# A two-block transformer on one core: the shared values' projection moved from behind the shared keys into the second attention

## The chip, the cores and the metric

One core of a Trainium2 chip runs the whole program in one launch. The metric is device time in microseconds (us); the kernel before takes 2057.99 us, the median of three runs (2056.74 to 2058.36). TensorE multiplies matrices, ScalarE and VectorE work elementwise, SyncE issues the weight transfers.

## The reference

A first block (two layers of gated branches) gives `x`, 256 tokens of width 1024 in float32. The second block, cut to what matters:

```python
def second_block(x, ...):
    h = x
    for layer in range(2):
        h = h + 0.5 * swiglu(rmsnorm(h, ffn1_norm[layer]), ...)
        hn = rmsnorm(h, mix_norm[layer])
        if layer == 0:
            h = h + mixer_a(hn, a_w_qkv, a_w_o, pos)
        else:
            h = h + mixer_b(hn, b_w_q, b_w_o, *shared, pos)
        h = h + 0.5 * swiglu(rmsnorm(h, ffn2_norm[layer]), ...)
        if layer == 0:
            shared = shared_kv(h, kv_norm, kv_w, pos)
    return rmsnorm(h, final_norm)

def shared_kv(h_stream, kv_norm, kv_w, pos):
    kv = rmsnorm(h_stream, kv_norm) @ kv_w       # 1024 x 2048, keys then values
    k, v = partial_rotary(kv[0], pos), kv[1]     # 16 heads of 64
```

`mixer_b` is causal attention over these keys and values with queries of its own (with 256 tokens there is one block of keys, so no selection), and `swiglu` is `(silu(h @ w_gate) * (h @ w_up)) @ w_down` with a hidden width of 2816. The shared keys and values come from `h` after layer 0; layer 1's first FFN starts from the same `h` under another norm.

## The kernel before, in words

**Weights.** All weights come as slots of 128 x 1024 numbers, in the order of use, through a ring of five buffers. A slot is loaded into `raw` (SyncE, once the slot five before it is used up), ScalarE copies it rounded into `w_hi` (line 1296), and VectorE subtracts to get the rest, `w_lo` (line 1808). Each product is made of three: high by high, high by low, low by high (lines 530 to 532). In the code of ScalarE and VectorE `split(c + AHEAD)` prepares slot c + 3, and `splits` several.

**Order.** There is no scheduler: the order on every engine is that of the code, and semaphores hold an engine at an instruction until another has counted up to a number. Whatever stands behind a waiting instruction on its engine waits too.

**Projection to tokens.** A block is four slots for 512 output columns. `wide_slot` multiplies one slot for both token tiles (twelve products of 512 columns), `wide` half of it, for one tile, into one accumulator bank per tile.

**Boundaries.** The residual stream is in `xt`, as four units (token tile x half of the width). At a boundary each unit is finished, turned by TensorE (`turn_unit`, line 914), multiplied by the norm's gains by VectorE (`gain_unit`, line 2212), rounded by ScalarE into the high part (`high_unit`, line 1512) and completed by VectorE with the low part (`low_unit`, line 2221). The row factor of the norm is applied later, to the results. Set 2 is for the shared keys and values (`kv_hi`, `kv_lo`, which lie in channels 4 to 11 of `g_hi`, `g_lo`), set 3, from the same `xt`, for layer 1's first FFN (`h_hi`, `h_lo`).

**Shared keys and values** (`keys_values`). Behind the boundary's first block of keys (k0) come a second block of keys (k1) and two of values (v0, v1). A key block is scaled by ScalarE (`take_tok`, line 1588), rotated by VectorE (`rope`, lines 2302 to 2305), turned by TensorE (`turn_qk`, line 1011) and copied out by ScalarE (`take_qk`, line 1595). A block of values is copied out, scaled, by VectorE (`take_values2`, line 2312). The four turned units of set 3 lie among these slots. Then follows the first block of FFN 2, which waits for all four:

```python
            keys_values()
            pe.wait_ge(v_ready, 3)
            pe.wait_ge(unit_lo, 4 * UNITS)
            wide_block(start["ffn2"], (0, 1))
```

**Second attention** (`attention_b`). Behind the queries' two blocks stand eight units of two heads. For each: scores (`scores2`, lines 1021 and 1022), bias and maximum on VectorE (`softmax2`, from line 2322), exponentials on ScalarE (`exps2`, lines 1603 and 1605), normalising on VectorE (`normalize2`, lines 2332 to 2336), the probabilities' transposes (`turn2`, line 1033), their copy by ScalarE (`take_turned2`, line 1611), products with the values (`values2`, line 1044), and the result's high part by ScalarE (`heads_high`, line 1615) and low part by VectorE (`heads_low`, line 2341). A unit's transposes wait until the unit before is through its low part. From unit 2 on, a unit's products stand in the middle of a slot of the output projection (`wo_slot`), and its transposes behind one. Units 0 and 1 have no projection around them.

Of the kernel before, what the change touches and what calls it, by code (L numbers as in the profile page):

```python
# [25 lines left out]
D = 1024  # L26
KD = D // P
BR = 512
# [8 lines left out]
AHEAD = 3  # L37
SEG = 3 * P
BLOCK = 4
UNITS = 4  # L40
# [46 lines left out]
def build(nc, weights, x_in, ctx_in, cols_in, consts_in, filter_consts_in, layer_in, filter_in, lam_in, tail_in, out):  # L87
# [8 lines left out]
    start = {}  # L96
# [22 lines left out]
    for p in (0, 2):  # L119
        start[f"pass{p}_merge"] = start[f"pass{p}"] + MERGE_AT  # L120
        start[f"pass{p}_wo"] = start[f"pass{p}"] + MERGE_AT + MERGE_SLOTS
    tail = [("ffn0", FFN_SLOTS), ("qkv", 24), ("wo0", 8), ("ffn1", FFN_SLOTS), ("kv", 16),
            ("ffn2", FFN_SLOTS), ("q1", 8), ("wo1", 8), ("ffn3", FFN_SLOTS)]
# [11 lines left out]
    with ctx:  # L135
# [392 lines left out]
        def _(pe):  # L528
# [606 lines left out]
            def keys_values():  # L1135

                c = start["kv"]
                k0, k1, v0, v1 = range(c, c + 16, BLOCK)
                wide_slot(k1, 0, (2, 3), kv_hi, kv_lo)
                turn_unit(3, 0, 6)  # L1140
                wide_slot(k1 + 1, 1, (2, 3), kv_hi, kv_lo)
                turn_qk(4, (0, 1))
                wide_slot(k1 + 2, 2, (2, 3), kv_hi, kv_lo)
                turn_unit(3, 1, 7)
                wide_slot(k1 + 3, 3, (2, 3), kv_hi, kv_lo)
                turn_unit(3, 2, 4)
                pe.wait_ge(qk_ready, 10)
                wide_slot(v0, 0, (0, 1), kv_hi, kv_lo)
                turn_unit(3, 3, 5)
                wide_slot(v0 + 1, 1, (0, 1), kv_hi, kv_lo)  # L1150
                turn_qk(5, (2, 3))
                wide_block(v0, (0, 1), 2, 4, kv_hi, kv_lo)
                pe.wait_ge(qk_ready, 12)
                wide_block(v1, (2, 3), 0, 4, kv_hi, kv_lo)

            def attention_b():

                qb = start["q1"] + BLOCK
# [7 lines left out]
                scores2(1, 2)  # L1166
                turn2(1, 0)

                values2(1, 0)
                scores2(1, 3)  # L1170
                turn_qk(7, (2, 3))
                turn2(1, 1)

                values2(1, 1)
                scores2(1, 4)
                turn2(1, 2)
                pe.wait_ge(qk_ready, 16)

                def values_scores(unit):
                    values2(1, unit)  # L1180
                    if unit + 3 < 8:
                        scores2(1, unit + 3)
                for i in range(6):
                    wo_slot(1, i, lambda: values_scores(i + 2))
                    if i + 3 < 8:
                        turn2(1, i + 3)
# [80 lines left out]
            keys_values()  # L1267
            pe.wait_ge(v_ready, 3)
            pe.wait_ge(unit_lo, 4 * UNITS)
            wide_block(start["ffn2"], (0, 1))  # L1270
            pe.wait_ge(v_ready, 4)
# [10 lines left out]
        def _(act):  # L1282
# [1478 lines left out]
```

## Time and profile before

| | |
|---|---|
| median of three runs | 2057.99 us |
| the profiled execution's own time | 2057.02 us |
| its span, first to last instruction | 2055.2 us |
| TensorE busy, of the span | 1983.5 us, 97% |
| VectorE, ScalarE busy | 1285.1 us (63%), 978.6 us (48%) |
| mean granted TensorE clock | 0.988 of full |
| TensorE on the chain that ended last | 88% |

Times in the trace count from the span's start. In a timeline a row gives an instruction's start and length; a bracket gives how long its engine stood idle ahead of it and whose work ended that. Consecutive instructions of an engine overlap a little, so the distance between two starts is what one of them costs. The granted clock is 1 at full speed and 0.5 at the lower of two levels; a stretch's figure is the mean over it. The shared keys and values stand at 1549 to 1595, the second attention at 1795 to 1856, behind it the boundary to the last FFN.

### The profile page before, as it was taken

How to read it: one execution, taken by the hardware profiler on the slowest of the kernel's cores; microseconds unless marked ns; L12 is line 12 of the kernel's file. 1: busy time of each engine (PE TensorE's matmuls, PEld its weight loads, DVE VectorE, ACT ScalarE, POOL GpSimd, SP SyncE). 2: the span in 40 equal slices, each digit the busy share in tenths (PEclk: the TensorE clock that was granted, in tenths of full speed). 3: DMA queues.
4: the chain of work that ended last, by engine and by line, in shares of the span. 5: the costliest groups of instructions: out<-in, count | busy, mean ns of one | idle time of the engine just before them, and what ended most of it. 6: DMA issues, size and time to landing. Idle time of an engine off the chain costs nothing.

```text
span 2055.2 us, 29618 instructions
## 1 busy us (share of the span) xinstructions
PE 1983.5 (97%) x12606; PEld 1717.9 (84%) x12606; DVE 1285.1 (63%) x1752; ACT 978.6 (48%) x1457; POOL 13.4 (1%) x18
## 2 busy tenths in 40 slices
PE   6999999999999999999989999999999999989998
PEld 3699999899998989999978887678888888768887
DVE  3777756887644777765565556755557555676555
ACT  1364444464333645534454446654445444565444
POOL 2000000000000000000000000000000000000000
PEclk9999999999999999999999999999999999999999
DMA  8544455434577443355545554345555555525654
GB/s 313 193 154 144 144 185 164 145 130 137 175 251 252 161 161 126 131 173 184 164 136 191 186 174 164 114 156 191 186 186 171 188 191 186 180 76 166 191 186 144
DMA packets 95491, 351.99 MB, mean 171 GB/s; under 512 B 10624, under 2 KB 10752, under 8 KB 94592
## 3 DMA queue, kind: packets, MB, share of 16 engines
q1 hardware_dynamic: 94032, 341.09, 50.2%
q0 software_dynamic: 1040, 7.37, 0.9%
q8 instruction: 100, 1.64, 0.3%
q10 hardware_dynamic: 288, 1.64, 0.2%
q14 instruction: 31, 0.25, 0.0%
HBM read 349.01 MB, written 1.05 MB: 170 GB/s over the span
## 4 chain that ended last, share of the span: by engine, by line
PE 88%; DVE 6%; ACT 3%; DMA 3%; issue 1%; SPq 0%; DVEq 0%; ACTq 0%
PE PS L530 26%; PE PS L532 25%; PE PS L531 25%; DMA raw<-weights 3%; DVE w_lo L1808 2%; ACT w_hi L1296 1%; PE PS L822 1%; PE PS L803 1%; PE PS L608 1%; PE PS L717 1%; PE PS L951 1%; PE PS L736 1%; PE PS L914 1%; PE PS L1033 1%; PE PS L726 0%
## 5 line engine op out<-in xcount | busy, mean ns | idle before, releaser
L1808 DVE TENSOR_TENSOR w_lo<-raw,w_hi 128x1024 fp32r<-128x1024 f32 x600 | 727.6, 1223 | 407.0 <-ACT w_hi L1296 405.4
L1296 ACT ACTIVATE w_hi<-raw 128x1024 fp32r<-128x1024 f32 x600 | 624.9, 1056 | 418.6 <-DMA raw<-weights 414.0
L530 PE MATMUL PS<-h_hi,w_hi 128*128 128x256 f32 x1568 | 454.6, 290 | 7.9 <-DVE h_lo L1826 3.9
L531 PE MATMUL PS<-h_lo,w_hi 128*128 128x256 f32 x1568 | 445.0, 284 | 0.0
L532 PE MATMUL PS<-h_hi,w_lo 128*128 128x256 f32 x1568 | 444.8, 284 | 0.0
L530 PE MATMUL PS<-w_hi,h_hi 128*128 128x512 f32 (+1 forms) x1024 | 388.8, 380 | 8.7 <-DVE h_lo L2171 6.5
L532 PE MATMUL PS<-w_hi,h_lo 128*128 128x512 f32 (+1 forms) x1024 | 380.0, 371 | 0.0
L531 PE MATMUL PS<-w_lo,h_hi 128*128 128x512 f32 (+1 forms) x1024 | 379.3, 370 | 0.0
L530 PEld LDWEIGHTS PS<-h_hi,w_hi 128*128 128x128 f32 x1568 | 301.7, 192 | 23.3 <-issue 16.9
L531 PEld LDWEIGHTS PS<-h_lo,w_hi 128*128 128x128 f32 x1568 | 302.1, 193 | 0.9 <-issue 0.7
L532 PEld LDWEIGHTS PS<-h_hi,w_lo 128*128 128x128 f32 x1568 | 301.8, 192 | 0.0
L530 PEld LDWEIGHTS PS<-w_hi,h_hi 128*128 128x128 f32 x1024 | 193.8, 189 | 44.9 <-issue 11.7
L532 PEld LDWEIGHTS PS<-w_hi,h_lo 128*128 128x128 f32 x1024 | 193.6, 189 | 33.6
L531 PEld LDWEIGHTS PS<-w_lo,h_hi 128*128 128x128 f32 x1024 | 194.0, 189 | 31.7 <-issue 1.2
L530 PE MATMUL PS<-w_hi,g_hi 128*128 128x512 f32 (+1 forms) x512 | 200.5, 392 | 2.2 <-issue 1.3
L532 PE MATMUL PS<-w_hi,g_lo 128*128 128x512 f32 (+1 forms) x512 | 196.4, 384 | 0.0
L531 PE MATMUL PS<-w_lo,g_hi 128*128 128x512 f32 (+1 forms) x512 | 196.1, 383 | 0.0
L530 PEld LDWEIGHTS PS<-w_hi,g_hi 128*128 128x128 f32 x512 | 96.3, 188 | 22.7 <-issue 4.3
L530 PE MATMUL PS<-g_hi,w_hi 128*128 128x256 f32 x384 | 111.5, 290 | 3.2 <-DVE g_lo L2136 1.6
L532 PEld LDWEIGHTS PS<-w_hi,g_lo 128*128 128x128 f32 x512 | 96.3, 188 | 19.2
L531 PEld LDWEIGHTS PS<-w_lo,g_hi 128*128 128x128 f32 x512 | 96.4, 188 | 17.3
L532 PE MATMUL PS<-g_hi,w_lo 128*128 128x256 f32 x384 | 109.4, 285 | 0.0
(258 smaller groups left out, 1879.8 us busy)
## 6 DMA issues: line engine op xcount, KB each, us to landing
raw<-weights SPq DMA_DIRECT2D x642, 512.0 KB, 3.4
x<-weights SPq DMA_DIRECT2D x6, 512.0 KB, 10.7
layer<-layer_in POOLq DMA_DIRECT2D x2, 1280.0 KB, 11.3
consts<-consts_in POOLq DMA_DIRECT2D x1, 1184.0 KB, 10.2
arena<-filter_consts_in ACTq DMA_DIRECT2D x1, 1024.0 KB, 8.8
cx<-ctx_in POOLq DMA_DIRECT2D x1, 1024.0 KB, 8.5
x<-x_in POOLq DMA_DIRECT2D x1, 1024.0 KB, 13.4
out<-arena SPq DMA_DIRECT2D x4, 256.0 KB, 2.0
```

The costliest lines, as they stand in the source:

```text
L530: pe.matmul(dst, hi, m_hi_, start=first, stop=False, **kw)
L531: pe.matmul(dst, hi, m_lo_, start=False, stop=False, **kw)
L532: return pe.matmul(dst, lo, m_hi_, start=False, stop=last, **kw)
L608: mm = pe.matmul(PS[32 * j:32 * j + 32, bank, 0:T], c_act[:, 4 * half + j, :], w[:, j * T:(j + 1) * T], start=(half == 0), stop=(half == 1))
L717: mm = pe.matmul(PS[:, SCORES + m, g * T:(g + 1) * T], q[s, h, qt * P:(qt + 1) * P], k[s, base + h, :], start=True, stop=True)
L736: mm = pe.matmul(PS[:, HEADS_OUT + qt, h * P:(h + 1) * P], mixw_t[:, h % 2, j, qt * P:(qt + 1) * P], v[:, t, h * P:(h + 1) * P], start=(j ...
L803: mm = pe.matmul(PS[:, [0, HEADS_OUT][n] + f, :], dft[:, t, f * P:(f + 1) * P], u_tok[:, t, :], start=(t == 0), stop=(t == 1))
L822: mm = pe.matmul(PS[:, [TURN, MISC][c // 2], (c % 2) * T:(c % 2 + 1) * T], yspec[:, a_, c * P:(c + 1) * P], idft[:, a_, :], start=(a_ == 0 ...
L914: mm = pe.transpose(PS[:, bank, j * P:(j + 1) * P], xt[:, t, kk * P:(kk + 1) * P], const("ident"))
L951: mm = pe.transpose(PS[:, 2 * (b % 2), o:o + P], act_f[:, t, f * P:(f + 1) * P], const("ident"))
L1296: nc.scalar.activation(w_hi[:, r, :], raw[:, r, :], ACT.Copy).then_inc(w_hi_ready, 1)
L1808: V.tensor_tensor(w_lo[:, r, :], raw[:, r, :], f32(w_hi[:, r, :]), ALU.subtract).then_inc(w_lo_ready, 1)
```

## The change

Three things are done. The values' two blocks (8 slots) leave the place behind the keys and stand in the second attention: v0 behind the queries' second block, with the transposes of unit 0 and of the queries among its slots, and v1 slot by slot around the products and scores of units 0 to 3. All output slots thereby move back: units 4 to 7 are in slots 0 to 3, and slots 4 and 5 are plain. The four units of set 3 are turned, gained and rounded earlier, among the second block of keys alone. The first block of FFN 2 follows these keys directly, and the transposes of the second keys stand inside it. The weights' order in memory follows.

```diff
-    tail = [("ffn0", FFN_SLOTS), ("qkv", 24), ("wo0", 8), ("ffn1", FFN_SLOTS), ("kv", 16),
-            ("ffn2", FFN_SLOTS), ("q1", 8), ("wo1", 8), ("ffn3", FFN_SLOTS)]
+    tail = [("ffn0", FFN_SLOTS), ("qkv", 24), ("wo0", 8), ("ffn1", FFN_SLOTS), ("kv", 8),
+            ("ffn2", FFN_SLOTS), ("q1", 8), ("kv_v", 8), ("wo1", 8), ("ffn3", FFN_SLOTS)]
...
-            def keys_values():
-
-                c = start["kv"]
-                k0, k1, v0, v1 = range(c, c + 16, BLOCK)
+            def keys_and_first_block():
+
+                k1, f0 = start["kv"] + BLOCK, start["ffn2"]
+                turn_unit(3, 0, 6)
+                turn_unit(3, 1, 7)
                 wide_slot(k1, 0, (2, 3), kv_hi, kv_lo)
-                turn_unit(3, 0, 6)
+                turn_unit(3, 2, 4)
                 wide_slot(k1 + 1, 1, (2, 3), kv_hi, kv_lo)
                 turn_qk(4, (0, 1))
+                turn_unit(3, 3, 5)
                 wide_slot(k1 + 2, 2, (2, 3), kv_hi, kv_lo)
-                turn_unit(3, 1, 7)
                 wide_slot(k1 + 3, 3, (2, 3), kv_hi, kv_lo)
-                turn_unit(3, 2, 4)
                 pe.wait_ge(qk_ready, 10)
-                wide_slot(v0, 0, (0, 1), kv_hi, kv_lo)
-                turn_unit(3, 3, 5)
-                wide_slot(v0 + 1, 1, (0, 1), kv_hi, kv_lo)
+                pe.wait_ge(unit_lo, 4 * UNITS)
+                wide_block(f0, (0, 1), 0, 2)
                 turn_qk(5, (2, 3))
-                wide_block(v0, (0, 1), 2, 4, kv_hi, kv_lo)
+                wide_block(f0, (0, 1), 2, 4)
                 pe.wait_ge(qk_ready, 12)
-                wide_block(v1, (2, 3), 0, 4, kv_hi, kv_lo)
 
             def attention_b():
 
-                qb = start["q1"] + BLOCK
+                qb, v0 = start["q1"] + BLOCK, start["kv_v"]
+                v1 = v0 + BLOCK
                 wide_slot(qb, 0, (2, 3))
                 turn_qk(6, (0, 1))
                 wide_slot(qb + 1, 1, (2, 3))
@@ -1164,26 +1163,34 @@
                 scores2(1, 1)
                 wide_slot(qb + 3, 3, (2, 3))
                 scores2(1, 2)
+
+                pe.wait_ge(qk_ready, 14)
+                wide_slot(v0, 0, (0, 1), kv_hi, kv_lo)
                 turn2(1, 0)
-
-                values2(1, 0)
-                scores2(1, 3)
+                wide_slot(v0 + 1, 1, (0, 1), kv_hi, kv_lo)
                 turn_qk(7, (2, 3))
-                turn2(1, 1)
-
-                values2(1, 1)
-                scores2(1, 4)
-                turn2(1, 2)
+                wide_block(v0, (0, 1), 2, 4, kv_hi, kv_lo)
                 pe.wait_ge(qk_ready, 16)
 
                 def values_scores(unit):
                     values2(1, unit)
                     if unit + 3 < 8:
                         scores2(1, unit + 3)
+
+                for unit in range(4):
+                    c = v1 + unit
+                    slot_ready(c)
+                    wide(c, unit, 0, 2, kv_hi, kv_lo)
+                    if unit == 0:
+                        pe.wait_ge(v_ready, 3)
+                    values_scores(unit)
+                    wide(c, unit, 1, 3, kv_hi, kv_lo).then_inc(w_used, 1)
+                    turn2(1, unit + 1)
+                pe.wait_ge(v_ready, 4)
                 for i in range(6):
-                    wo_slot(1, i, lambda: values_scores(i + 2))
-                    if i + 3 < 8:
-                        turn2(1, i + 3)
+                    wo_slot(1, i, lambda: values_scores(i + 4) if i < 4 else None)
+                    if i < 3:
+                        turn2(1, i + 5)
...
-            keys_values()
-            pe.wait_ge(v_ready, 3)
-            pe.wait_ge(unit_lo, 4 * UNITS)
-            wide_block(start["ffn2"], (0, 1))
-            pe.wait_ge(v_ready, 4)
+            keys_and_first_block()
...
-            def keys_values():
-
-                c = start["kv"]
-                k0, k1, v0, v1 = range(c, c + 16, BLOCK)
+            def keys_and_first_block():
+
+                k0, f0 = start["kv"], start["ffn2"]
+                k1 = k0 + BLOCK
                 take_tok(4, k0, (0, 1), 3)
-                splits(k1, 2)
                 high_unit(3, 0)
+                split(k1 + AHEAD)
+                high_unit(3, 1)
+                split(k1 + 1 + AHEAD)
                 take_qk(4, k[:, 0:4, :], (0, 1))
+                high_unit(3, 2)
                 split(k1 + 2 + AHEAD)
-                high_unit(3, 1)
+                high_unit(3, 3)
                 split(k1 + 3 + AHEAD)
-                high_unit(3, 2)
                 take_tok(5, k1, (2, 3), 3)
-                split(v0 + AHEAD)
-                high_unit(3, 3)
-                split(v0 + 1 + AHEAD)
+                splits(f0, 2)
                 take_qk(5, k[:, 4:8, :], (2, 3))
-                splits(v0 + 2, 2)
-                splits(v1, 4)
-                splits(start["ffn2"], 4)
+                splits(f0 + 2, 2)
...
+                split(v0 + AHEAD)
                 take_turned2(1, 0)
-                heads_high(1, 0)
                 exps2(1, 2)
+                split(v0 + 1 + AHEAD)
                 take_qk(7, q[:, 4:8, :], (2, 3))
-                take_turned2(1, 1)
-                heads_high(1, 1)
-                exps2(1, 3)
-                wo = start["wo1"]
-                for unit in range(2, 8):
-                    take_turned2(1, unit)
-                    split(wo + unit - 2 + AHEAD)
+                splits(v0 + 2, 2)
+                for unit in range(8):
+                    if unit >= 1:
+                        take_turned2(1, unit)
+                    split((v1 + unit if unit < 4 else wo + unit - 4) + AHEAD)
                     heads_high(1, unit)
-                    if unit + 2 < 8:
+                    if 1 <= unit < 6:
                         exps2(1, unit + 2)
-                split(wo + 6 + AHEAD)
+                splits(wo + 4, 3)
...
-            def keys_values():
-
-                c = start["kv"]
-                k0, k1, v0, v1 = range(c, c + 16, BLOCK)
+            def keys_and_first_block():
+
+                k0, f0 = start["kv"], start["ffn2"]
+                k1 = k0 + BLOCK
+                gain_unit(3, 0, 6)
                 rope(4)
                 split(k1 + AHEAD)
-                gain_unit(3, 0, 6)
+                gain_unit(3, 1, 7)
+                low_unit(3, 0)
                 split(k1 + 1 + AHEAD)
-                low_unit(3, 0)
+                gain_unit(3, 2, 4)
+                low_unit(3, 1)
                 split(k1 + 2 + AHEAD)
-                gain_unit(3, 1, 7)
-                split(k1 + 3 + AHEAD)
-                low_unit(3, 1)
-                gain_unit(3, 2, 4)
-                rope(5)
-                split(v0 + AHEAD)
                 gain_unit(3, 3, 5)
                 low_unit(3, 2)
-                split(v0 + 1 + AHEAD)
+                split(k1 + 3 + AHEAD)
                 low_unit(3, 3)
-                splits(v0 + 2, 2)
-                take_values2(v0, (0, 1), 0, 3)
-                splits(v1, 4)
-                take_values2(v1, (2, 3), 1, 3)
-                splits(start["ffn2"], 4)
+                rope(5)
+                splits(f0, 4)
...
-
+                rope(7)
+                split(v0 + AHEAD)
                 softmax(2)
-                rope(7)
+                split(v0 + 1 + AHEAD)
                 normalize2(1, 1)
-                heads_low(1, 0)
-                softmax(3)
-                normalize2(1, 2)
-                heads_low(1, 1)
-                wo = start["wo1"]
-                for unit in range(2, 8):
-                    if unit + 2 < 8:
+                splits(v0 + 2, 2)
+                take_values2(v0, (0, 1), 0, 3)
+                for unit in range(8):
+                    if unit == 4:
+                        take_values2(v1, (2, 3), 1, 3)
+                    if 3 <= unit + 2 < 8:
                         softmax(unit + 2)
-                    split(wo + unit - 2 + AHEAD)
-                    if unit + 1 < 8:
+                    split((v1 + unit if unit < 4 else wo + unit - 4) + AHEAD)
+                    if 2 <= unit + 1 < 8:
                         normalize2(1, unit + 1)
                     heads_low(1, unit)
-                split(wo + 6 + AHEAD)
+                splits(wo + 4, 3)
```

What it makes of the rows of an engine is shown at three places. First VectorE behind the boundary to the keys, 12 rows from the key block's rope on; `w_lo<-raw,w_hi` is a split, `arena<-PS,cols` a gain and `h_lo<-arena,h_hi` a low part of set 3, and `arena<-arena,consts` begins a rope. Before:

```order
L1808 TENSOR_TENSOR w_lo<-raw,w_hi 128x1024 [waits w_hi_ready]
L2212 TENSOR_TENSOR arena<-PS,cols 128x512 [waits unit_turned]
L1808 TENSOR_TENSOR w_lo<-raw,w_hi 128x1024 [waits w_hi_ready]
L2221 TENSOR_TENSOR h_lo<-arena,h_hi 128x4x128 [waits unit_hi]
L1808 TENSOR_TENSOR w_lo<-raw,w_hi 128x1024 [waits w_hi_ready]
L2212 TENSOR_TENSOR arena<-PS,cols 128x512 [waits unit_turned]
L1808 TENSOR_TENSOR w_lo<-raw,w_hi 128x1024 [waits w_hi_ready]
L2221 TENSOR_TENSOR h_lo<-arena,h_hi 128x4x128 [waits unit_hi]
L2212 TENSOR_TENSOR arena<-PS,cols 128x512 [waits unit_turned]
L2302 TENSOR_TENSOR arena<-arena,consts 128x256 [waits tok_ready]
L2303 TENSOR_TENSOR arena<-arena,consts 128x16x8
L2304 TENSOR_TENSOR arena<-arena,consts 128x16x8
```

And now (the line numbers are one higher):

```order
L1809 TENSOR_TENSOR w_lo<-raw,w_hi 128x1024 [waits w_hi_ready]
L2213 TENSOR_TENSOR arena<-PS,cols 128x512 [waits unit_turned]
L2222 TENSOR_TENSOR h_lo<-arena,h_hi 128x4x128 [waits unit_hi]
L1809 TENSOR_TENSOR w_lo<-raw,w_hi 128x1024 [waits w_hi_ready]
L2213 TENSOR_TENSOR arena<-PS,cols 128x512 [waits unit_turned]
L2222 TENSOR_TENSOR h_lo<-arena,h_hi 128x4x128 [waits unit_hi]
L1809 TENSOR_TENSOR w_lo<-raw,w_hi 128x1024 [waits w_hi_ready]
L2213 TENSOR_TENSOR arena<-PS,cols 128x512 [waits unit_turned]
L2222 TENSOR_TENSOR h_lo<-arena,h_hi 128x4x128 [waits unit_hi]
L1809 TENSOR_TENSOR w_lo<-raw,w_hi 128x1024 [waits w_hi_ready]
L2222 TENSOR_TENSOR h_lo<-arena,h_hi 128x4x128 [waits unit_hi]
L2303 TENSOR_TENSOR arena<-arena,consts 128x256 [waits tok_ready]
```

All four gains and low parts stand within four splits now, and the second keys' rope behind the last of them; before, two low parts stood in these rows, and the rope ahead of the others.

Second TensorE in the second attention, where the first values are used; `PS<-arena,v` are products with the values, `PS<-qk` scores, `PS<-consts,arena` transposes of probabilities. Before, from the last product of the queries' second block:

```order
L532 MATMUL PS<-w_hi,h_lo 128x512
L1021 MATMUL PS<-qk 128x128 [waits qk_ready,biased_ready]
L1022 MATMUL PS<-qk 128x256
L1021 MATMUL PS<-qk 128x128
L1022 MATMUL PS<-qk 128x256
L1033 MATMUL PS<-consts,arena 128x128 [waits o2_ready,p2t_ready,p2n_ready]
L1033 MATMUL PS<-consts,arena 128x128 x5
L1044 MATMUL PS<-arena,v 64x128 [waits p2t_ready]
L1044 MATMUL PS<-arena,v 64x128 x5
L1021 MATMUL PS<-qk 128x128 [waits qk_ready,biased_ready]
```

And now, in the first slot of v1:

```order
L531 MATMUL PS<-w_lo,g_hi 128x512
L532 MATMUL PS<-w_hi,g_lo 128x512
L1044 MATMUL PS<-arena,v 64x128 [waits p2t_ready,v_ready]
L1044 MATMUL PS<-arena,v 64x128 x5
L1021 MATMUL PS<-qk 128x128 [waits qk_ready,biased_ready]
L1022 MATMUL PS<-qk 128x256
L1021 MATMUL PS<-qk 128x128
L1022 MATMUL PS<-qk 128x256
L530 MATMUL PS<-w_hi,g_hi 128x512
```

The first products with the values now have half a weight slot ahead of and behind them, and a wait for `v_ready`, which before was met at the FFN.

Third VectorE around the copy of the first block of values (`v<-PS,stat`). Before, in the shared values:

```order
L2221 TENSOR_TENSOR h_lo<-arena,h_hi 128x4x128 [waits unit_hi]
L1808 TENSOR_TENSOR w_lo<-raw,w_hi 128x1024 [waits w_hi_ready] x2
L2312 TENSOR_SCALAR v<-PS,stat 128x512 [waits w_used]
L2312 TENSOR_SCALAR v<-PS,stat 128x512
L1808 TENSOR_TENSOR w_lo<-raw,w_hi 128x1024 [waits w_hi_ready] x4
L2312 TENSOR_SCALAR v<-PS,stat 128x512 [waits w_used]
L2312 TENSOR_SCALAR v<-PS,stat 128x512
```

And now, in the second attention:

```order
L1809 TENSOR_TENSOR w_lo<-raw,w_hi 128x1024 [waits w_hi_ready]
L2333 RECIPROCAL stat<-stat 128x4 [waits p2_ready]
L2336 TENSOR_SCALAR arena<-arena,stat 128x128 [waits dve_chain]
L2337 TENSOR_SCALAR arena<-arena,stat 128x256
L2336 TENSOR_SCALAR arena<-arena,stat 128x128
L2337 TENSOR_SCALAR arena<-arena,stat 128x256
L1809 TENSOR_TENSOR w_lo<-raw,w_hi 128x1024 [waits w_hi_ready] x2
L2313 TENSOR_SCALAR v<-PS,stat 128x512 [waits w_used]
L2313 TENSOR_SCALAR v<-PS,stat 128x512
L1809 TENSOR_TENSOR w_lo<-raw,w_hi 128x1024 [waits w_hi_ready]
L2342 TENSOR_TENSOR g_lo<-PS,g_hi 128x256 [waits o2_hi]
```

The copy now stands behind a split, the normalising of unit 1 and two further splits.

## Rows read from the trace of the kernel before

**Rows 1.** Who TensorE waited for, 1795 to 1870: us, times, longest us.

```profile
PE PS L1044 <- ACT arena L1611: 3.1, 2, 2.2
...
PE PS L1033 <- DVE arena L2336: 1.4, 1, 1.4
```

**Rows 2.** Stretches: us, PE, PEld, DVE, ACT, POOL busy (instructions), PEclk, DMA share, GB/s.

```profile
1000.00:1020.00 20.00, 17.28 (x131) 16.82 (x130) 10.74 (x17) 8.80 (x16) 0.00 (x0) 0.91 0.45 150
...
1275.00:1295.00 20.00, 17.39 (x103) 13.11 (x100) 13.96 (x30) 10.57 (x25) 0.00 (x0) 1.00 0.35 120
...
1560.00:1580.00 20.00, 20.00 (x106) 16.68 (x105) 13.80 (x21) 11.42 (x17) 0.00 (x0) 1.00 0.53 172
...
1809.50:1823.50 14.00, 9.19 (x68) 6.44 (x68) 11.88 (x34) 9.54 (x28) 0.00 (x0) 0.76 0.11 39
```

**Rows 3.** Timeline, TensorE, shared keys: start us, us, engine, line, operation, count.

```profile
1558.56 0.39 PE L530 MATMUL PS<-w_hi,g_hi 128*128 128x512 f32 x1
...
1561.28 0.60 PE L914 MATMUL PS<-consts,cx 128*128 128x128 f32 x4
...
1561.63 0.48 PE L530 MATMUL PS<-w_hi,g_hi 128*128 128x512 f32 x1
...
1564.49 1.04 PE L1011 MATMUL PS<-consts,arena 128*128 128x128 f32 x8
...
1565.28 0.47 PE L530 MATMUL PS<-w_hi,g_hi 128*128 128x512 f32 x1
```

**Rows 4.** Timeline, VectorE, shared keys and values.

```profile
1560.36 1.23 DVE L1808 TENSOR_TENSOR w_lo<-raw,w_hi 128x1024 fp32r<-128x1024 f32 x1 [0.85 <-ACT w_hi L1296]
...
1563.83 0.69 DVE L2212 TENSOR_TENSOR arena<-PS,cols 128x512 f32<-128x512 f32 x1
...
1584.56 1.41 DVE L2312 TENSOR_SCALAR v<-PS,stat 128x512 f32<-128x512 f32 x2
```

**Rows 5.** Timeline, ScalarE, shared keys.

```profile
1564.39 1.06 ACT L1296 ACTIVATE w_hi<-raw 128x1024 fp32r<-128x1024 f32 x1 [2.05 <-DMA raw<-weights]
...
1565.36 0.62 ACT L1512 ACTIVATE h_hi<-arena 128x512 fp32r<-128x512 f32 x1
```

**Rows 6.** Timeline, TensorE, second attention; brackets: idle before, and releaser.

```profile
1809.76 0.50 PE L1021 MATMUL PS<-qk 64*128 64x128 f32 x4 [0.53 <-DVE arena L2322]
...
1812.14 1.39 PE L1033 MATMUL PS<-consts,arena 128*128 128x128 f32 x6 [1.44 <-DVE arena L2336]
...
1815.69 1.55 PE L1044 MATMUL PS<-arena,v 128*64 128x128 f32 x12 [2.16 <-ACT arena L1611]
...
1825.80 0.88 PE L1044 MATMUL PS<-arena,v 128*64 128x128 f32 x12
...
1845.81 0.85 PE L1033 MATMUL PS<-consts,arena 128*128 128x128 f32 x6 [0.89 <-DVE g_lo L2341]
...
1851.32 0.85 PE L1033 MATMUL PS<-consts,arena 128*128 128x128 f32 x6 [0.88 <-DVE g_lo L2341]
```

**Rows 7.** Timeline, VectorE, second attention.

```profile
1813.83 1.23 DVE L1808 TENSOR_TENSOR w_lo<-raw,w_hi 128x1024 fp32r<-128x1024 f32 x1 [1.75 <-ACT w_hi L1296]
...
1814.97 0.95 DVE L2322 SCALAR_TENSOR_TENSOR arena<-PS,layer 128x768 f32<-128x768 f32 x1
...
1817.08 0.42 DVE L2302 TENSOR_TENSOR arena<-arena,consts 128x256 f32<-128x256 f32 x1
...
1818.28 0.17 DVE L2332 RECIPROCAL stat<-stat 128x4 f32<-128x4 f32 x1
...
1819.41 0.42 DVE L2341 TENSOR_TENSOR g_lo<-PS,g_hi 128x256 fp32r<-128x256 f32 x1
```

**Rows 8.** Timeline, ScalarE, second attention.

```profile
1817.56 0.39 ACT L1603 ACTIVATE arena<-arena,stat 128x128 f32<-128x128 f32 x1
...
1819.62 1.09 ACT L1595 ACTIVATE qk<-PS 128x512 f32<-128x512 f32 x2 [0.21 <-PE PS L1011]
```

**Rows 9.** Timeline, TensorE, boundary behind the first attention.

```profile
1354.58 0.66 PE L914 MATMUL PS<-consts,cx 128*128 128x128 f32 x4 [0.87 <-DVE cx L2205]
```

More of the change, by code:

```diff
@@ L1667, in attention_a @@
                 splits(wo + 4, 3)
-            def keys_values():
-                c = start["kv"]
-                k0, k1, v0, v1 = range(c, c + 16, BLOCK)
+            def keys_and_first_block():
+                k0, f0 = start["kv"], start["ffn2"]
+                k1 = k0 + BLOCK
                 take_tok(4, k0, (0, 1), 3)
-                splits(k1, 2)
                 high_unit(3, 0)
+                split(k1 + AHEAD)
+                high_unit(3, 1)
+                split(k1 + 1 + AHEAD)
                 take_qk(4, k[:, 0:4, :], (0, 1))
+                high_unit(3, 2)
                 split(k1 + 2 + AHEAD)
-                high_unit(3, 1)
+                high_unit(3, 3)
                 split(k1 + 3 + AHEAD)
-                high_unit(3, 2)
                 take_tok(5, k1, (2, 3), 3)
-                split(v0 + AHEAD)
-                high_unit(3, 3)
-                split(v0 + 1 + AHEAD)
+                splits(f0, 2)
                 take_qk(5, k[:, 4:8, :], (2, 3))
-                splits(v0 + 2, 2)
-                splits(v1, 4)
-                splits(start["ffn2"], 4)
+                splits(f0 + 2, 2)
             def attention_b():
-                qb = start["q1"] + BLOCK
+                qb, v0 = start["q1"] + BLOCK, start["kv_v"]
+                v1, wo = v0 + BLOCK, start["wo1"]
                 take_tok(6, qb - BLOCK, (0, 1), 4)
@@ L1779, in _ @@
             boundary(3, 2, start["kv"])
-            keys_values()
+            keys_and_first_block()
             ffn_rest(2)
@@ L2423, in softmax @@
                     softmax2(1, unit, "bias_causal")
-                qb = start["q1"] + BLOCK
+                qb, v0 = start["q1"] + BLOCK, start["kv_v"]
+                v1, wo = v0 + BLOCK, start["wo1"]
                 rope(6)
@@ L2523, in _ @@
             boundary(lambda u: down_unit(1, u), 3, 2, start["kv"], (2, 3, 4, 5))
-            keys_values()
+            keys_and_first_block()
             ffn_rest(2)
@@ L2693, in pack @@
     ffn(2, 0)
-    for c in range(0, 2 * D, BR):
+    for c in range(0, D, BR):
         wide(g["kv_w_2"][:, c:c + BR])
@@ L2698, in pack @@
         wide(g["b_w_q_2"][0][:, c:c + BR])
+    for c in range(D, 2 * D, BR):
+        wide(g["kv_w_2"][:, c:c + BR])
     summed(g["b_w_o_2"][0])
```

## The prediction

> **What bounds the kernel now.** I read the busy shares first, then who TensorE waits for, then the clock by stretches, and last the three engines' rows in the two places that the change touches. TensorE is busy for 97% of the span, so time can be won or lost only where it stands idle or runs at the lower clock. In the shared keys and values it does neither: 20.00 us busy of 20.00, clock 1.00 [rows 2]. In the second attention it waits 3.1 us for ScalarE's copies of turned probabilities and 1.4 us for the first probabilities [rows 1], and in the 14 us from 1809.50 the granted clock is 0.76 [rows 2]: 14 x 0.24 x 2 = 6.7 us at the lower of its two levels (1.2 instead of 2.4 GHz). Its output there shows it: six transposes take 1.39 us at 1812.14 and 0.85 at 1845.81, a unit's value products 1.55 us at 1815.69 and 0.88 at 1825.80 [rows 6].
>
> **What the change can win.** It lays eight slots of value projection (12 products each, 2.72 us, from 1558.56 to 1561.28 [rows 3]), 21.8 us of the same work, from after the keys to the second attention: no cost as such, only other neighbours. Two whole slots now stand between the third scores, the first transposes and the turn of the second queries, two more behind those, and four stand halved about units 0 to 3. The idle of 1.44 and 2.16 us [rows 6] and the other 0.9 of the 3.1 us [rows 1] get work in front of them: 4.5 us. Without those gaps the low stretch should go too. Its price, by the same instructions at both clocks: transposes 1.39 - 0.85 = 0.54, products 1.55 - 0.88 = 0.67, and about the same again for the two pieces behind them (scores, turn of queries), which I take at 1.0; 2.2 us together. At most 4.5 + 2.2 = 6.7 us. The gaps of 0.89 and 0.88 us ahead of the last two units' transposes [rows 6] stay: they come of a chain of 5.51 us per unit (transpose, ScalarE's copy, split, VectorE's split, normalising, low parts), which the change doesn't shorten.
>
> **New wait one: the next norm's units behind the keys.** Before, the four units of the next norm were turned among keys and values and were needed only 16 slots after the boundary. Now the first FFN slot stands behind four key slots and waits for all four units' low parts. I walk both sides from what isn't moved. TensorE: the first key block ends at 1558.56; two turns (0.35 each), four slots (three at 2.86, from 1561.63 to 1564.49, one at 2.72), two more turns and the turn of the keys (0.8, from 1564.49 to 1565.28) [rows 3] give 1558.56 + 0.7 + 11.3 + 1.5 = 1572.1. VectorE: the last untouched split starts at 1560.36 [rows 4] and is followed 1.14 us later (as at 1813.83 and 1814.97 [rows 7]) by the first gain, at 1561.50. From then each unit is a ring through two engines: gain 0.69 [rows 4] and 0.03 to hand over; ScalarE's high part 0.62, of which 0.54 until its next instruction [rows 5]; its weight split 1.06 and the hand-over, 1.08; VectorE's weight split, 1.14; then the next gain: 3.48 us. The rope of the keys (1.2 us, from 1817.08 to 1818.28 [rows 7]) fits beside the first. The fourth gain starts at 1561.50 + 3 x 3.48 = 1571.94; 3.48 later comes its low part, after VectorE's split, not ahead of it, and 0.68 later it is there: 1576.1. TensorE waits 4.0 us, or 4.1 with the hand-over. Weights don't shorten or lengthen this: the first FFN slot's had landed by 1564.39, where ScalarE stopped waiting for it [rows 5], and the ring asks for them at 1566.2. Bounds: 3.0 if hand-overs vanish and splits overlap better, 4.8 if they cost double. Behind the waiting slot TensorE has the turn of the second keys, which nothing waits for this early.
>
> **New wait two: the first half of the values.** TensorE reaches unit 0's first half slot at about 1825.1: third scores end at 1810.7 (the 1.44 us ahead of 1812.14 [rows 6]); slot 2.9; transposes 0.6; slot 2.8; turn of queries 0.85; two slots 5.5; 0.3 for the fifth slot's split, below; half a slot 1.4. There it waits for the values to be taken out of the accumulator. VectorE's order ahead of that copy: a split at 1813.83, 1.14 [rows 7]; rope 1.2, to 1816.2; split 1.14; softmax of unit 2, 2.1 (1814.97 to 1817.08 [rows 7]), to 1819.4. Then ScalarE: exponentials 1.8 (1817.56 to 1819.41 [rows 8]), split 1.06, to 1822.4; VectorE's split of the fifth slot starts only there and ends at 1823.6 (TensorE, ready at 1823.4, loses 0.3); normalising 1.13 (1818.28 to 1819.41 [rows 7]); two splits, 2.3, to 1827.0; and the copy itself, 1.41 [rows 4], to 1828.4. So 1828.4 - 1825.1 = 3.3, with the 0.3 it is 3.5 us; bounds 2.5 and 4.5. Queued behind the wait are the products of unit 0, and on them ScalarE's and VectorE's high and low parts, so the unit ring of 5.51 us starts late by all of it.
>
> **Smaller terms.** The second half of the values is copied at the head of unit 4, 1.41 us, with TensorE waiting ahead of the output projection while only transposes (0.6) cover it: +0.85; bounds 0.4 and 1.5, since the copy also delays that unit's softmax. The last two output slots now stand bare, and VectorE's three trailing splits run into the boundary. The first attention ends in that form already, and the turn there waits 0.87 us [rows 9]; at the second attention's end there is no such wait among TensorE's [rows 1]: +0.9, bounds 0 and 1.
>
> **The clock.** No row shows a gap of 3.3 or 4 us here. In 1000 to 1020 TensorE stands idle for 2.7 us (17.28 busy of 20) and the clock is 0.91, so 3.5 us low; in 1275 to 1295 idle for 2.6 us (17.39 busy) and the clock is 1.00 [rows 2]. Gaps of 4.1 and 3.3 are longer than the one that was punished. I count one such stretch behind each, 3.5 us of work at half speed less a little that falls into the gap: 1.5 us each, 3.0 together; bounds 0 and 2.2 each, the latter the price of the longer stretch above. The Trainium skill (TensorE: Matmul & The Clock Gate, Part 1) says that the monitor runs free of the program, so that one kernel finds different amounts of its work cold in different runs. By that page these two terms could be missing or whole in any run; the two stretches just compared, alike in idle and unlike in clock, agree.
>
> **The sum.** -6.7 + 4.1 + 3.5 + 0.85 + 0.9 + 3.0 = +5.7 us. The profiled execution took 2057.02 (its span 2055.2), so 2062.7; the median of the runs shown, 2057.99, lies 0.97 above it, which gives **2063.6**. A change under 0.2%, 4.1 us, counts as none here, as about what a measurement of this kernel can tell.
>
> **Rivals.**
> - The waits come, the clock holds (or only one is punished): +2.7 to +4.1, 2061. For it: the stretch from 1275. Against: the one from 1000, and 6.7 us at the lower level about gaps of only 0.53, 1.44 and 2.16 us [rows 6]. 0.16.
> - Wait one comes as above, wait two doesn't, because ScalarE gets to the fifth slot's split before TensorE needs anything: -6.7 + 4.1 + 0.85 + 0.9 + 1.5 = +0.7, 2058.7. 0.10. Against it: the exponentials stand ahead of that split in ScalarE's order.
> - The other side, faster: both engines keep ahead and the projection covers all. It decides at two points: the fourth unit's low part is there by 1572.1, and the values by 1825.1. Then -6.7 + 0.85 + 0.9 = -5, 2053. For it: in the keys ScalarE and VectorE are busy only 11.42 and 13.80 us of 20 [rows 2]. Against it: that idle time is the ring's own, each waiting for the other, and the ring is what the wait is for. 0.10.
> - Worse: each gap brings a long low stretch as that at 1812 (2.2 instead of 1.5), and the copy of the second values puts VectorE behind for each later unit, 0.6 us for three units: 5.7 + 1.4 + 1.8 = +9, 2067. 0.08.
> - My forecast, +4.2 to +8: 0.56.
>
> **Range and chances.** 2058.3 to 2067 holds the forecast, the first two rivals and an edge of the last; outside lie the fast case and the rest. Slower by over 0.2%: 0.56 + 0.08 = 0.64. Within: 0.16 and most of 0.10, 0.25. Faster: 0.11.
>
> **What would show it.** In the profile after: a wait of the first FFN product behind the keys for VectorE's low parts of h, some 4 us; a wait of the first value products for VectorE's copy of v, some 3.3 us; the waits for turned probabilities and for the first probabilities gone; the clock near 1.00 where it was 0.76, and under 1 for some 3.5 us behind each new wait; a turn at the end of the attention waiting 0.9 us. It is wrong if either new wait is under 2 us, or if the clock holds behind both.

## The result and the profile after

The changed kernel takes 2065.11 us, the median of six runs (2063.13 to 2068.82), against 2058.18 for the kernel before, measured with it (2056.74 to 2059.19): a ratio of 1.0036, 95% interval 1.0023 to 1.0049, so 6.9 us slower. The profiled execution took 2064.77, its span 2062.9, against 2057.02 and 2055.2.

Whom TensorE waited for, from 1540 to 1600, in the profile after (us in total, times, longest us):

```profile
PE PS L530 <- issue: 3.9, 1, 3.9
PE PS L914 <- DVE cx L2196: 0.4, 1, 0.4
```

And from 1795 to 1900:

```profile
PE PS L1044 <- DVE v L2313: 3.0, 1, 3.0
PE PS L1033 <- DVE g_lo L2342: 1.8, 2, 0.9
PE PS L914 <- DVE cx L2206: 0.9, 1, 0.9
PE PS L530 <- DVE v L2313: 0.7, 1, 0.7
...
PE PS L530 <- DVE w_lo L1809: 0.4, 1, 0.4
```

The 3.1 and 1.4 us of [rows 1] are gone. In their place stand the values' copy, its second half, and the turn at the last boundary, which is the size of [rows 9]. The first list shows the largest new wait as "issue", with no releaser: the waiting product has three semaphores to wait for, and who it was is seen only by laying the engines' rows side by side. TensorE:

```profile
1560.33 1.03 PE L914 MATMUL PS<-consts,cx 128*128 128x128 f32 x8
...
1578.00 0.47 PE L530 MATMUL PS<-w_hi,h_hi 128*128 128x512 f32 x1 [3.93 <-issue]
...
1813.95 0.88 PE L1044 MATMUL PS<-arena,v 128*64 128x128 f32 x12 [3.00 <-DVE v L2313]
1814.76 0.80 PE L1021 MATMUL PS<-qk 64*128 64x128 f32 x4
1815.35 1.07 PE L1022 MATMUL PS<-qk 64*128 64x256 f32 x4
...
1866.13 0.66 PE L914 MATMUL PS<-consts,cx 128*128 128x128 f32 x4 [0.89 <-DVE cx L2206]
```

VectorE, behind the first key block:

```profile
1563.32 0.68 DVE L2213 TENSOR_TENSOR arena<-PS,cols 128x512 f32<-128x512 f32 x1
...
1566.79 0.68 DVE L2213 TENSOR_TENSOR arena<-PS,cols 128x512 f32<-128x512 f32 x1
...
1576.07 1.23 DVE L1809 TENSOR_TENSOR w_lo<-raw,w_hi 128x1024 fp32r<-128x1024 f32 x1 [1.05 <-ACT w_hi L1299]
1577.22 0.68 DVE L2222 TENSOR_TENSOR h_lo<-arena,h_hi 128x512 fp32r<-128x512 f32 x1
```

The gains are 3.47 us apart, and the fourth low part, behind a split that itself waited 1.05 us for ScalarE, ends at 1577.90; the product starts at 1578.00. VectorE, in the second attention:

```profile
1807.95 1.23 DVE L1809 TENSOR_TENSOR w_lo<-raw,w_hi 128x1024 fp32r<-128x1024 f32 x1 [2.88 <-ACT w_hi L1299]
...
1810.22 2.36 DVE L1809 TENSOR_TENSOR w_lo<-raw,w_hi 128x1024 fp32r<-128x1024 f32 x2
1812.49 1.41 DVE L2313 TENSOR_SCALAR v<-PS,stat 128x512 f32<-128x512 f32 x2
```

The copy of v ends at 1813.90, the products start at 1813.95. The clock behind the two waits, as stretches (columns as in [rows 2]):

```profile
1575.00:1585.00 10.00, 7.00 (x24) 5.64 (x25) 5.29 (x9) 4.09 (x6) 0.00 (x0) 0.83 0.30 97
1808.00:1822.00 14.00, 10.62 (x67) 7.53 (x67) 10.27 (x17) 6.16 (x10) 0.00 (x0) 0.88 0.30 104
```

10 x 0.17 x 2 and 14 x 0.12 x 2 are 3.4 us each at the lower level, one stretch behind each wait; TensorE had been idle for 3.93 and 3.00 us before.

**Where the time went.** I cut the span at three starts: A, the end of the first key block; B, the queries' first turn; C, the first turn of the last boundary. (Before, A is [rows 3]'s first row, B stands at 1797.77 and C at 1858.51; after, they are 1560.33, 1783.28 and 1866.13.) Eight slots of 2.72 us, 21.8 us, have moved from A-B to B-C.

| kernel | to A | A to B | B to C | A to C |
|---|---|---|---|---|
| before | 1558.56 | 239.21 | 60.74 | 299.95 |
| after | 1560.33 | 222.95 | 82.85 | 305.80 |
| after minus before, the eight moved slots taken out | | +5.5 | +0.3 | +5.85 |

From C on, both need 196.7 and 196.8. So the stretch with the keys lost 5.5 us, the one with the attention 0.3, and 1.8 us lie ahead of A, where both kernels do the same work.

### The profile page after: what moved, and what is told of

It reads as the page before. It is cut to its first block, busy times and chain, and to the rows that moved or that the text cites. A ratio compares the mean times of both kernels' runs of the same rounds, so it can differ in the third digit from the quotient of the medians.

```text
span 2062.9 us, 29619 instructions
## 1 busy us (share of the span) xinstructions
PE 1989.1 (96%) x12606; PEld 1718.9 (83%) x12606; DVE 1285.4 (62%) x1752; ACT 977.5 (47%) x1457; POOL 13.4 (1%) x18
## 3 DMA queue, kind: packets, MB, share of 16 engines
HBM read 349.01 MB, written 1.05 MB: 170 GB/s over the span
## 4 chain that ended last, share of the span: by engine, by line
PE 86%; DVE 7%; DMA 3%; ACT 3%; issue 1%; SPq 0%; DVEq 0%; ACTq 0%
PE PS L530 26%; PE PS L532 25%; PE PS L531 25%; DMA raw<-weights 3%; DVE w_lo L1809 2%; ACT w_hi L1299 1%; PE PS L608 1%; PE PS L822 1%; PE PS L803 1%; PE PS L717 1%; PE PS L951 1%; PE PS L736 1%; PE PS L914 1%; PE PS L1033 1%; PE PS L664 0%
## 5 line engine op out<-in xcount | busy, mean ns | idle before, releaser
L531 PE MATMUL PS<-g_lo,w_hi 128*128 128x256 f32 x384 | 108.6, 283 | 0.0
```

The costliest lines, as they stand in the source:

```text
L531: pe.matmul(dst, hi, m_lo_, start=False, stop=False, **kw)
```

## The experiments

All lists of waits are TensorE's. Ratios are to the kernel before, measured together with each.

**Undoing the first wait.**

```diff
 # VectorE (ScalarE and TensorE alike)
-gain_unit(3, 0, 6); rope(4)
-split(k1 + AHEAD);     gain_unit(3, 1, 7); low_unit(3, 0)
-split(k1 + 1 + AHEAD); gain_unit(3, 2, 4); low_unit(3, 1)
-split(k1 + 2 + AHEAD); gain_unit(3, 3, 5); low_unit(3, 2)
-split(k1 + 3 + AHEAD); low_unit(3, 3)
+gain_unit(3, 0, 6); gain_unit(3, 1, 7); low_unit(3, 0); low_unit(3, 1)
+rope(4)
+gain_unit(3, 2, 4); gain_unit(3, 3, 5); split(k1 + AHEAD)
+low_unit(3, 2); low_unit(3, 3)
+split(k1 + 1 + AHEAD); split(k1 + 2 + AHEAD); split(k1 + 3 + AHEAD)
```

> The changed kernel, but the next norm's four units go ahead of the weight splits behind the shared keys: gains, high parts and low parts of units 0 and 1 directly behind each other, then the keys' rope, then units 2 and 3 with one split between; only then the other splits. The second attention is left as changed. My theory (the first FFN slot waits 3.9 us because the units run in a ring of 3.48 us with the splits, and the lower clock behind it costs 1.5 us): that wait is under 0.3 us, no low stretch there, and 2065.1 - 3.9 - 1.5 = 2059.7 us. Rival (splits that now come later are what TensorE waits for next): a wait for w_lo of some 3 us in the same place and 2064 to 2065 us.

Measured 2057.99 us (2056.47 to 2060.68), ratio 1.0000 (0.9992 to 1.0009). From 1558 to 1600 the list of waits is empty. A to B is 216.78 us, 6.2 less than after, where my theory had 5.4; with the first wait undone, the changed kernel equals the one before in time. Of the four splits behind the keys the first two came 2.7 and 1.5 us later than in the changed kernel (counted from A), the last two earlier, and TensorE waited for none: the rival falls.

**Undoing the second wait.**

```diff
 # VectorE
 normalize2(1, 1)
-splits(v0 + 2, 2)
 take_values2(v0, (0, 1), 0, 3)
+splits(v0 + 2, 2)
 # ScalarE
 take_turned2(1, 0)
-exps2(1, 2)
 split(v0 + 1 + AHEAD)
+exps2(1, 2)
```

> The changed kernel, but in the second attention VectorE copies out the first block of values ahead of the two splits that stood before it, and ScalarE splits the fifth slot before the exponentials of unit 2, not behind. The keys are left as changed. My theory (3.0 us of wait for the values, 0.4 for the fifth slot, 1.5 for the clock behind them): both waits under 0.3 us, 2065.1 - 4.9 = 2060.2 us. Rival (the values' place in the attention costs by itself, VectorE has too much to do there, and the wait only moves on to the first transposes or the next slot's split): the waits of TensorE between the third scores and unit 2 still sum to over 2.5 us, 2063 to 2065 us.

Measured 2059.50 us (2057.11 to 2061.99), ratio 1.0008 (1.0000 to 1.0017). Waits in the attention from 1790 on:

```profile
PE PS L1033 <- DVE g_lo L2342: 2.2, 3, 0.9
PE PS L914 <- DVE cx L2206: 0.9, 1, 0.9
PE PS L530 <- DVE v L2313: 0.6, 1, 0.6
PE PS L1021 <- DVE arena L2323: 0.5, 1, 0.5
```

Both waits are gone, for 0.49 us more at unit 1's transposes (the first line has a third entry). That is all between the third scores and unit 2, so the rival falls. VectorE's copy now waits 1.63 us for TensorE, not the reverse:

```profile
1810.27 1.41 DVE L2313 TENSOR_SCALAR v<-PS,stat 128x512 f32<-128x512 f32 x2 [1.63 <-PE PS L532]
```

B to C is 78.42 us, 4.4 less than after. The first wait, which this kernel keeps, is 4.10 us, also under the name "issue".

**Both.** The same two edits together.

> Both reorderings at once, on the keys and in the second attention. My theory: the terms add, 2065.1 - 5.4 - 4.9 = 2054.8 us, 3.4 us faster than the kernel before, since the old waits of 4.5 us and the old low stretch of 2.2 us are won and only 0.65 and 0.9 us of new waits stay. Rival (the two waits hide a common cost, such as the weights' arrival, so that they don't add): 2058 to 2060 us.

Measured 2054.00 us (2049.32 to 2058.59), ratio 0.9975 (0.9961 to 0.9989). A to B is 216.99, B to C 78.25, A to C 295.24. That is 10.56 less than after, where the two edits alone had saved 6.17 and 4.43, 10.60 together: the terms add.

**Filling the gaps.** Throw-away products while TensorE waits:

```diff
 pe.wait_ge(qk_ready, 10)
+for _ in range(16):
+    pe.matmul(PS[:, 0, :], kv_hi[:, 0, 0:P], <512 columns of kv_hi>, start=True, stop=True)
 pe.wait_ge(unit_lo, 4 * UNITS)
...
 if unit == 0:
+    for _ in range(12):
+        pe.matmul(PS[:, 3, :], kv_hi[:, 0, 0:P], <the same>, start=True, stop=True)
     pe.wait_ge(v_ready, 3)
```

> The changed kernel with all its waits in place, but TensorE does throw-away products (512 columns) in the two new gaps: 16 ahead of the first FFN slot behind the keys, 12 ahead of unit 0's products with the values, into accumulator banks that are overwritten next. They bring nothing but a busy TensorE, and should fit inside the gaps (3.6 of 3.9 us, 2.7 of 3.0). My theory of the clock: no stretch at the lower level behind either gap, 1.5 us saved at each, 2065.1 - 3.0 = 2062.1 us. Rival (the gaps alone are the cost and the lower clock behind them falls on work that is waiting anyway): 2065 us, the same as without them.

Measured 2060.99 us (2056.50 to 2064.66), ratio 1.0017 (1.0008 to 1.0027). The median is 4.1 us below the changed kernel's, where my theory had 3.0 and the rival none; but the changed kernel's interval, 1.0023 to 1.0049, just overlaps this one, so the trace has to decide. The clock stays up:

```profile
1573.00:1585.00 12.00, 11.90 (x57) 9.60 (x56) 6.03 (x10) 6.21 (x9) 0.00 (x0) 1.00 0.38 131
1805.00:1819.00 14.00, 13.33 (x85) 9.69 (x85) 11.76 (x24) 7.21 (x16) 0.00 (x0) 1.00 0.25 80
```

The first FFN product starts 17.52 us behind A (after: 17.67) and the first products with the values 30.64 behind B (after: 30.67), so the fillers delayed nothing; A to B is 221.00 and B to C 81.40, 1.95 and 1.45 less than after. That is the low clock's price, 3.4 us for both by one profile of each kernel; the waits cost the rest.

**The second half of the values.**

```diff
-pe.wait_ge(v_ready, 4)
 for i in range(6):
-    wo_slot(1, i, lambda: values_scores(i + 4) if i < 4 else None)
+    wo_slot(1, i, lambda: behind_half(i))   # waits for v_ready 4 when i == 0, then the same
```

> Both reorderings as in the run with both, and TensorE's wait for the second block of values moved from ahead of the output projection's first slot to the middle of it, ahead of unit 4's products. My theory (VectorE's copy of 1.41 us at the head of unit 4 makes that unit's ring late, 0.65 us of wait are only where it shows first): the wait goes but the next transposes come no earlier, 6.3 us after the ones before instead of 5.5, and the time stays within 0.3 us of 2054.0. Rival (the wait's place is the cost): 0.65 us less, 2053.3.

Measured 2054.67 us (2050.84 to 2058.38), ratio 0.9982 (0.9973 to 0.9991). The wait turned into one of 0.79 us at the next transposes, and these stay 6.29 us behind the ones before:

```profile
1827.75 0.85 PE L1033 MATMUL PS<-consts,arena 128*128 128x128 f32 x6
1834.04 0.85 PE L1033 MATMUL PS<-consts,arena 128*128 128x128 f32 x6 [0.79 <-DVE g_lo L2346]
```

VectorE's copy in the unit's ring is the cost, not the place where TensorE notices it. The time lies 0.7 us from the 2054.0 of the run with both, more than the 0.3 I had allowed, but the intervals of the two kernels overlap.

**The late split.** As the last, and:

```diff
 # VectorE, end of attention_b; then the boundary
-splits(wo + 4, 3)
+splits(wo + 4, 2)
 def unit_and_split(u):
     wo_unit(1, u)
+    if u == 0:
+        split(start["wo1"] + 6 + AHEAD)
-boundary(lambda u: wo_unit(1, u), ...)
+boundary(unit_and_split, ...)
```

> As the half-wait kernel, and VectorE's last trailing split behind the second attention goes behind the first finished unit of the boundary, where it idled 0.7 us. My theory (that split in front of the first unit is the 0.7 to 0.9 us for which TensorE's first turn waits): that wait is under 0.3 us and the time 0.5 to 0.7 less than with the half wait alone. Rival (the split only moves the wait to the second turn or to the next norm's low parts): no change.

Measured 2051.96 us (2050.21 to 2055.07), ratio 0.9970 (0.9961 to 0.9980). The turn's wait is gone from the list, B to C is 77.39, 1.1 less than with the half wait alone. The medians differ by more, 2.7 us, which one such wait doesn't explain; their intervals overlap.

**Filling the old gaps.** Throw-away products in the kernel before:

```diff
 scores2(1, 2)
+fill(6)
 turn2(1, 0)
+fill(8)
 values2(1, 0)
...
 turn2(1, 1)
+fill(3)
 values2(1, 1)
```

> The kernel before, but TensorE does throw-away products (512 columns) in the three gaps of the second attention's units 0 and 1: 6, 8 and 3 of them, into an accumulator bank that is free there, 3.9 us of the 4.5. All waits stay. My theory (the clock's low stretch there costs 2.2 us besides the gaps): the granted clock is 1.00 in that stretch, the transposes of unit 0 take 0.85 us instead of 1.39, and the time is 2.2 us less than before's, 2056. Rival (the low stretch falls on work that waits anyway, so the term of 2.2 us in my sum is wrong and something else made up for it): 2058.

Measured 2059.40 us (2054.48 to 2061.09), ratio 1.0003 (0.9994 to 1.0013): nothing gained, though the clock stayed at 1.00:

```profile
1807.00:1822.00 15.00, 11.81 (x89) 8.11 (x88) 12.87 (x36) 9.97 (x30) 0.00 (x0) 1.00 0.11 36
```

TensorE's rows, in which B is 1795.96:

```profile
1813.87 0.88 PE L1044 MATMUL PS<-arena,v 128*64 128x128 f32 x12 [0.83 <-ACT arena L1618]
...
1816.60 1.09 PE L1011 MATMUL PS<-consts,arena 128*128 128x128 f32 x8 [0.99 <-DVE arena L2312]
1818.16 0.85 PE L1033 MATMUL PS<-consts,arena 128*128 128x128 f32 x6 [0.46 <-DVE g_lo L2348]
...
1821.81 0.85 PE L1033 MATMUL PS<-consts,arena 128*128 128x128 f32 x6 [0.17 <-DVE g_lo L2348]
```

The same points in the kernel before, in which B is 1797.77:

```profile
1818.76 1.27 PE L1011 MATMUL PS<-consts,arena 128*128 128x128 f32 x8
1819.97 0.85 PE L1033 MATMUL PS<-consts,arena 128*128 128x128 f32 x6
...
1823.63 0.85 PE L1033 MATMUL PS<-consts,arena 128*128 128x128 f32 x6 [0.17 <-DVE g_lo L2341]
```

Counted from B, unit 0's transposes start at 14.35 us (before: 14.37) and its products with the values at 17.91 (before: 17.92), so the fillers delayed nothing here either. At full speed the products are done sooner, and TensorE then waits for the rope (0.99) and for low parts (0.46), which it had not waited for while it was slow. The third unit's transposes stand 25.85 us behind B in one and 25.86 in the other, B to C is 60.74 in both. My theory fell.

**The front.** The kernels before and after, unaltered, for further profiles:

> The changed kernel once more, unaltered, on the chip of this call. My theory (the change costs 5.9 us between the shared keys and the last boundary, and the 1.8 us more that its first profile showed ahead of the shared keys come of the execution and not of the change): 5 to 7 us over the kernel before, the first turn behind the first key block anywhere from 1558.5 to 1562, and from there to the first turn of the last boundary the same 305.8 us as before within 0.5. Rival (the change slows the unchanged front too, by the new place of its weights or its instructions): the front is again 1.5 us or more longer than the kernel before's 1558.6, and the whole over 7 us slower.

> The kernel before once more, unaltered, for another profile. My theory (the time up to the end of the first key block, in code that no kernel here changes, spreads over several us from one execution to the next): that point lies between 1557 and 1562 us, and from there to the first turn of the last boundary it is 299.95 us within 0.4. Rival (the kernel before is steadily faster in front than the changed one): 1557 to 1559.

> The same as the run before it, a third profile of the kernel before; the same expectations.

> A third profile of the changed kernel. My theory: the end of the first key block between 1557 and 1562 us, and from there 305.8 us within 0.4. Rival (a front slower by the change): 1560 to 1562, as in the two profiles so far.

The changed kernel again, five runs: 2065.97 us (2065.13 to 2067.66), ratio 1.0040 (1.0027 to 1.0052). That is 7.1 us over the kernel before measured with it, and its front (A at 1561.68) was 3.1 us longer than 1558.6: taken alone, both spoke for the rival. The other three, one run each, gave 2059.84, 2059.84 and 2064.97 us. (Where the expectation says "the same 305.8 as before", the changed kernel's first profile is meant.) By their profiles:

| kernel | to A | A to C |
|---|---|---|
| before, three profiles | 1558.56, 1560.55, 1561.94 | 299.95, 300.75, 299.36 |
| after, three profiles | 1560.33, 1561.68, 1560.04 | 305.80, 305.74, 306.38 |

In front of A the means are 1560.35 and 1560.68, and the kernel before was itself up to 3.4 us later than in its first profile: the rival falls, and the 1.8 us of the first pair are the execution's. (Three profiles of each can't exclude a difference of some tenths.) From A to C they are 300.02 and 305.97, 5.95 apart. The spread of A to C, up to 0.7 from the mean, was larger than the 0.4 I had allowed; the values of the last three profiles (300.75, 299.36, 306.38) all fell outside what I had written down. The long profile of the kernel before, 300.75, shows where it comes from: its low stretch began later and fell on the queries' turn and unit 1's transposes, which then took 1.97 and 1.38 us:

```profile
1820.46 1.97 PE L1011 MATMUL PS<-consts,arena 128*128 128x128 f32 x8
1822.22 1.38 PE L1033 MATMUL PS<-consts,arena 128*128 128x128 f32 x6
```

and unit 2's transposes stand 26.96 us behind B instead of 25.86. So in this one profile the low stretch of the kernel before did cost time, 1.1 us.

Part of the spread ahead of A can be read too. In the first attention, which no kernel so far changes, TensorE waits 2.57 to 2.61 us ahead of unit 0's transposes in all profiles. The kernel before, in its first profile and its third:

```profile
1280.81 0.88 PE L1033 MATMUL PS<-consts,arena 128*128 128x128 f32 x6 [2.61 <-DVE arena L2336]
```

```profile
1283.43 1.54 PE L1033 MATMUL PS<-consts,arena 128*128 128x128 f32 x6 [2.57 <-DVE arena L2336]
```

In the first the clock stays at 1.00 there ([rows 2]), in the third it is at the lower level for 3.4 us and the same six transposes take 1.54 us. The stretch of the third:

```profile
1275.00:1295.00 20.00, 16.90 (x89) 12.66 (x88) 12.66 (x26) 10.56 (x25) 0.00 (x0) 0.91 0.34 110
```

Of the thirteen profiles up to here, five have such a stretch at this gap: the third of the kernel before, the third of the changed kernel, and those of the kernels with the first wait undone, with the second wait undone and with the half wait. From these transposes to the turn of [rows 9] it is 75.01 to 75.28 us in the five and 73.67 to 73.82 in the eight others: 1.4 us, given or taken by the clock in unchanged code.

That the full difference of medians, 6.9 and 7.1 us, is about 1 us more than 5.95 stays open; it is within the intervals.

**The late split in both attentions.**

```diff
 # VectorE, end of attention_a; the boundary as above
-splits(wo + 4, 3)
+splits(wo + 4, 2)
```

> As the late-split kernel, with the same move of VectorE's last trailing split at the end of the first attention too. My theory: the wait of 0.87 us there is under 0.3, and the time 0.6 to 0.9 less than the late-split kernel's, 2051.2. Rival (the first attention's end is held by something else): 2052.

Measured 2050.26 us (2048.85 to 2054.20), ratio 0.9963 (0.9950 to 0.9977). The turn there no longer waits, and from the first attention's unit 0 transposes to it there are 72.70 us, 1.0 less than the 73.67 to 73.82 above; the rival falls. By the medians the kernel is 1.7 us faster than the late-split one, but the two intervals overlap, so the times alone don't show it. This is the fastest version, some 8 us faster than the kernel before and 15 than the changed one, by the order of instructions alone.

## Why the prediction was right

The forecast was 2063.6 us, +5.7 in the profile's terms; the cut from A to C gives +5.85, over three profiles +5.95. By place the forecast had +5.6 at the keys (wait and clock) and nearly nothing in the attention; measured were +5.5 and +0.3. The measured median, 2065.11, lies 1.5 us above the forecast; about 1 us of it is the part of the 6.9 us that isn't found between A and C, and its cause stays open. Put in as measured, the terms below give -6.7 + 3.93 + 3.38 + 0.65 + 0.89 + 3.4 = +5.55, so no large error was hidden by another.

- **Wait one**: 4.1 forecast, 3.93 measured (4.05, 4.10 and 4.20 in other profiles), by the ring of 3.48 us forecast and 3.47 found. Undoing the order took it away.
- **Wait two**: 3.5 forecast, 3.00 and 0.38 measured. The walk had TensorE arrive 27.3 us behind B and start at 30.6; it arrived at 27.7 and started at 30.67, 0.05 behind the end of VectorE's copy.
- **Second half of the values**: 0.85 forecast, 0.65 measured as a wait. I had priced the wait where TensorE shows it; what costs is that the ring of unit 4 was 6.3 us instead of 5.5, and moving the wait won nothing.
- **The boundary**: 0.9 forecast, 0.89 measured.
- **The clock behind the waits**: 3.0 forecast, 3.4 by the filled gaps. Each of the two waits had its low stretch in all three profiles of the changed kernel, 3.4 us long but for one of 6.8 us at the first wait, which began while TensorE still waited. Of the Trainium skill's sentence (TensorE: Matmul & The Clock Gate, Part 1) that one kernel finds different amounts of its work cold in different runs, I had said that two stretches of one run agree with it. Two places of one run can't show that. The fourteen profiles do, at the place from 1275 that I had taken as unpunished: the gap of 2.6 us there was followed by a low stretch in five of them. The gap of 2.62 us at the other place, from 1000, was followed by one in all fourteen, and so were the long waits here: for these the variation didn't come.
- **The clock before, 2.2 us of the 6.7 to be won**: this step failed in its reason. As time in which TensorE did less than it can, the 2.2 us were there and the change did win them. But in the profile they were read from they were no price of the clock: with the clock up and the old order kept, B to C stayed at 60.74 us. (Where the stretch came later, in the second profile, 1.1 us of it were.) From the third scores to unit 2's transposes the old section ran at the pace of ScalarE and VectorE (take the queries, split, softmax, rope, normalise), and slow products merely filled what would have been more waiting. The change won them by putting weight slots there, not by keeping the clock. The size of the term came out right for another reason than the one I gave; for a change that only keeps the clock, it would have promised up to 2.2 us that aren't there.
- **The fast rival** needed both chains to run ahead; the two reorderings make exactly that come true, and give 2054.0 where I had put the rival at 2053.

## What to carry to other kernels

Moving work into a stage with idle time wins that idle time only if what the engine needs next is ready when the moved work ends: walk the producers' in-order queues up to that instruction, and put what is waited for ahead of the weight splits that have slack. A slow clock costs what it seems only where the slowed engine sets the pace; filling a gap with throw-away products, and comparing the stage with and without them, tells the two apart. And a wait that has lost its partner in the list ("issue") is found by laying the producers' rows beside it.

## What the runs showed of the hardware

TensorE stood idle for 3.0 to 4.2 us in eight places of five profiles (two in each of the changed kernel's three, one in each of the two kernels with one reordering), and each time 3.4 us or more at the lower clock came with it. Where this was taken away by keeping TensorE busy with useless products, the clock stayed at 1.00 and the two parts of the span, A to B and B to C, were 1.95 and 1.45 us shorter. A gap of 2.6 us in unchanged code was followed by such a stretch in five of fourteen profiles, another of 2.62 us in all fourteen, so the length of the wait alone doesn't tell.

In unchanged code, up to A, thirteen executions of nine kernels spread from 1557.1 to 1563.5 us. Two single profiles can thus differ by several us without any cause in the change; cutting the span at points around the changed stages left 0.7 us of spread from the mean.
